# Gated delta rule: the inverse of the chunk triangle from 16x16 blocks instead of 8x8, and the side work of a head in another order

## What is computed

```python
def _gated_delta(q, k, v, beta, g):            # per head, in chunks of 64 tokens
    gc = jnp.cumsum(chunks(g), axis=-1)
    decay = jnp.where(incl, jnp.exp(jnp.where(incl, diff, 0.0)), 0.0)
    kb = k * beta[..., None]
    lower = jnp.where(strict, jnp.einsum('bhncd,bhned->bhnce', kb, k) * decay, 0.0)
    tri = lower + jnp.eye(GDN_CHUNK)
    rhs = jnp.concatenate([v * beta[..., None], kb * jnp.exp(gc)[..., None]], axis=-1)
    sol = lax.linalg.triangular_solve(tri, rhs, left_side=True, lower=True, unit_diagonal=True)
    u, w = sol[..., :d], sol[..., d:]
    intra = jnp.einsum('bhncd,bhned->bhnce', q, k) * decay
    def step(state, xs):
        v_new = u_i - w_i @ state
        o = qh_i @ state + intra_i @ v_new
        state = state * exp(gl_i) + kt_i.T @ v_new
```

## Time and profile before

| | |
|---|---|
| median of three runs | 2551.5 us (2549.22 to 2552.22) |
| the profiled execution: its own time | 2552.11 us |
| its span, first to last instruction | 2550.3 us |
| mean granted PE clock | 0.979 of full |
| busy: PE, POOL, DVE, ACT | 2360.8, 1320.1, 1397.3, 591.1 us |
| gated-delta stages | about 577 to 995 us and 1783 to 2197 us of the span |
| moved from and to HBM | 316 MB, 124 GB/s on average |

### The profile page before, as it was taken

One profiled execution on the slowest core, in us unless ns is written; L12 is line 12 of the kernel. 1 busy time (PEld: TensorE's weight loads), 2 busy tenths in 40 slices (PEclk: granted clock), 3 DMA queues, 4 the chain that ended last, 5 costly groups with the idle time before them and its releaser, 6 DMA issues.

```text
span 2550.3 us, 36954 instructions
## 1 busy us (share of the span) xinstructions
PE 2360.8 (93%) x13312; PEld 1891.9 (74%) x13312; DVE 1397.3 (55%) x2112; ACT 591.1 (23%) x1150; POOL 1320.1 (52%) x1018
## 2 busy tenths in 40 slices
PE   0898999998999999999998999999899999999996
PEld 0666777786777777777876788788677777887885
DVE  8964654656666664665126255155666665234536
ACT  0211210222223332222023122022222222224001
POOL 6673357434444444656655644644444444554763
PEclk9998999998999999999999999999999999999998
DMA  9864346321122213454325532532122222222542
GB/s 360 303 218 168 117 157 249 127 93 58 60 67 67 67 61 120 150 190 162 98 68 200 179 116 94 198 110 78 57 67 67 67 67 67 67 83 67 182 141 91
DMA packets 94595, 316.01 MB, mean 124 GB/s; under 512 B 10918, under 2 KB 11174, under 8 KB 93382
## 3 DMA queue, kind: packets, MB, share of 16 engines
q1 hardware_dynamic: 86768, 295.48, 33.7%
q10 hardware_dynamic: 7644, 18.16, 2.1%
HBM read 303.89 MB, written 8.39 MB: 122 GB/s over the span
## 4 chain that ended last, share of the span: by engine, by line
PE 71%; DVE 16%; POOLq 3%; ACT 3%; issue 3%; DMA 2%; POOL 1%; DVEq 1%; ACTq 1%; SPq 0%
PE bank L651 14%; PE bank L653 14%; PE bank L652 14%; DVE arena L1709 12%; PE bank L1172 4%; PE bank L1174 4%; PE bank L1173 4%; DVE acc L1709 3%; PE bank L961 2%; PE bank L932 2%; ACT arena L1202 1%; POOLq L1651 1%; POOL w_lo L1649 1%; PE bank L953 1%; DVEq L1710 1%
## 5 line engine op out<-in xcount | busy, mean ns | idle before, releaser
L1645 POOL CAST w_hi<-ring 128x1024 fp32r<-128x1024 f32 (+1 forms) x320 | 353.8, 1106 | 1098.5 <-PE bank L653 916.0
L1649 POOL TENSOR_TENSOR w_lo<-ring,w_hi 128x512 fp32r<-128x512 f32 (+1 forms) x632 | 885.1, 1421 | 48.5 <-issue 1.3
L651 PE MATMUL bank<-h_hi,w_hi 128*128 128x512 f32 x1952 | 826.5, 423 | 10.3 <-POOLq L1651 8.4
L653 PE MATMUL bank<-h_hi,w_lo 128*128 128x512 f32 x1952 | 773.1, 396 | 0.0
L652 PE MATMUL bank<-h_lo,w_hi 128*128 128x512 f32 x1952 | 769.5, 394 | 0.0
L651 PEld LDWEIGHTS bank<-h_hi,w_hi 128*128 128x128 f32 x1952 | 372.7, 191 | 95.4 <-issue 15.6
L653 PEld LDWEIGHTS bank<-h_hi,w_lo 128*128 128x128 f32 x1952 | 371.2, 190 | 84.6
L652 PEld LDWEIGHTS bank<-h_lo,w_hi 128*128 128x128 f32 x1952 | 373.0, 191 | 72.5 <-issue 7.2
L1202 ACT ACTIVATE arena<-bank 128x512 f32<-128x512 f32 (+5 forms) x360 | 169.3, 470 | 668.9 <-PE bank L653 216.6
L1709 DVE SCALAR_TENSOR_TENSOR acc<-yT,cact,acc 128x1024 f32<-128x1024 f32 (+1 forms) x144 | 209.6, 1455 | 37.3 <-DMA acc<-in_b_mod 14.2
L1172 PE MATMUL bank<-w_hi,h_hi 128*128 128x512 f32 x448 | 175.6, 392 | 0.5 <-issue 0.5
(11 more groups left out here) (230 smaller groups left out, 2828.4 us busy)
## 6 DMA issues: line engine op xcount, KB each, us to landing
ring<-in_stream SPq DMA_DIRECT2D x352, 512.0 KB, 3.5
yT<-in_stream SPq DMA_DIRECT2D x128, 512.0 KB, 4.6
yT<-in_mod SPq DMA_DIRECT2D x32, 1024.0 KB, 7.9
arena<-in_x ACTq DMA_DIRECT2D x4, 1024.0 KB, 9.7
x_norm<-arena ACTq DMA_DIRECT2D x4, 1024.0 KB, 8.1
arena<-x_norm ACTq DMA_DIRECT2D x4, 1024.0 KB, 10.0
out<-arena SPq DMA_DIRECT2D x3, 1024.0 KB, 3.9
arena<-in_x SPq DMA_DIRECT2D x1, 2048.0 KB, 13.9
```

What stands on the lines that cost most here:

```text
L651: mm(PJ[b][:, :], hi, h_hi[:, k, :], start=(k == 0), stop=False)
L653: last = mm(PJ[b][:, :], lo, h_hi[:, k, :], start=False, stop=(k == KT - 1))
L1645: pool.tensor_copy(w_hi[:, par, 0:w], ring[:, slot, 0:w])
L1649: pool.tensor_tensor(w_lo[:, par, at], ring[:, slot, at], w_hi[:, par, at].bitcast(F32), ALU.subtract)
```

## The change

It makes the substitution over 16x16 blocks: 14 steps instead of 6, on tiles of 16 columns for each chunk. The level of 8 is dropped, so PE, ACT and DVE merge twice, and then once more for the whole chunk. The running inverse and the broadcast row lie in a PSUM bank, TB[1], which has held the key product until then; the reduced triangle and the products lie in the second half of `A(14)`. The copies `lT_swapped`, which nobody reads, are gone.

The order of the side work is another. On DVE, the substitution stands directly behind the triangle; `intra`, `mask(1)` and `both_squares` stand behind the assembly; the tail of the head before stands behind the first update; v and `conv_k0` behind the second; `conv_k1` behind the `own` copies; the scaling of v behind the `cross` block; the coefficients of the next head are copied by a part of their own (`coef`) behind that; `key` and `weigh` stand at the end of the recurrence. On PE, the turning of `intra` (`gdn_iT`) and the tail of the head before are moved behind the first update and the second product, the turning of v to `REC - 2`; the fill is another, 25 k-steps between the key product and the first merge, 2 in the recurrence where there were 3. On ACT, the tail stands behind the copy of the first product, with the tanh of v behind it; the copy of `intra`, the tanh of z and the square of q stand behind the second product; ACT's copy of w waits for DVE's product with z; `tanh_q` and `norm_k` come one chunk later.

```diff
-BASE = 8
-LEVELS = (8, 16, 32)
+BASE = 16
+LEVELS = (16, 32)
...
         base_l, base_x, base_row, base_part = (
-            A(11)[:, NW + i * NB:NW + (i + 1) * NB].rearrange("p (t n) -> p t n", t=TT) for i in range(4))
-        lT_n, lT_swapped = narrow(A(12)), narrow(A(12)[:, NW:])
+            ap[:, i * NB:(i + 1) * NB].rearrange("p (t n) -> p t n", t=TT)
+            for ap, i in ((A(14)[:, NW:], 0), (TB[1], 0), (TB[1], 1), (A(14)[:, NW:], 1)))
+        lT_n, lv_n = narrow(A(12)), narrow(A(12)[:, NW:])
...
-        gdn_fill = [5, 6, 5] + [3, 3, 2, 3, 2, 3, 2, 3, 2] + [2, 3, 2, 3, 3, 3, 3, 3, 3]
+        gdn_fill = [5, 9, 9] + [7, 3, 2, 3, 2, 3, 2] + [2, 2, 2, 2, 3, 2, 2, 2, 2]
...
                         if s == 1:
-                            ready("gdn_egb")
                             ready("gdn_lower")
                             transposes(MB, A(3)).then_inc(S("gdn_lT"), 1)
-                            if not first:
-                                tail(h - 1)
-                        if s == 2:
-                            ready("gdn_lT_copied")
-                            ready("gdn_intra")
-                            transposes(MB, A(17)).then_inc(S("gdn_iT"), 1)
...
+                                if v == len(LEVELS) - 1:
+
+                                    pe.wait_ge(S("gdn_T"), D * 2 * len(LEVELS) + 2 * v + 1)
+                                    transposes(MB, A(17)).then_inc(S("gdn_iT"), 1)
...
-                                if v == 1:
-
-                                    pe.wait_ge(S("y_ready"), after("y_ready", l * 16 + NSA_H + h))
-                                    ready("gdn_v")
-                                    transposes(OB, A(10)).then_inc(S("gdn_vT"), 1)
+                                if v == 0 and not first:
+                                    ready("gdn_egb")
+                                    tail(h - 1)
...
                                 if v == 0:
+                                    if not first:
+                                        tail(h - 1)
+                                    act.wait_ge(S("gdn_conv"), D * 3 + 3)
+                                    fn(A(5), A(10), ACT.Tanh, scale=0.5).then_inc(S("gdn_vtanh"), 1)
+                                if v == len(LEVELS) - 1:
+                                    ready("gdn_iT")
+                                    fn(A(16), MB[:, :], ACT.Copy).then_inc(S("gdn_i_copied"), 1)
+                                    fn(A(18), raw[:, 3, TAPS - 1:], ACT.Tanh, scale=0.5).then_inc(S("gdn_ztanh"), 1)
                                     front(h, "square_q")
-                                if v == 2 and not last:
+                                if v == N_LEVELS - 1 and not last:
                                     front(h + 1, "tanh_k")
                         if s == REC - 1:
                             ready("gdn_w")
+                            act.wait_ge(S("raw_used3"), after("raw_used3", l * N_LOTS + h + 1))
                             fn(A(18), TB[0][:, :], ACT.Copy, scale=-1.0).then_inc(S("gdn_w_copied"), 1)
...
                     tt(A(3), TB[1][:, :], A(2), M).then_inc(S("gdn_lower"), 1)
-                    if not first:
-                        both_squares(h - 1)
-                    ready("gdn_qk")
-                    tt(A(17), SB_[0][:, :], A(17), M).then_inc(S("gdn_intra"), 1)
-
-
-                    tt(tiles(A(14)), tiles(A(3)), over(C("base_lower").unsqueeze(1), BIG), M)
-                    reduce(base_l, A(14).rearrange("p (t b n) -> p t n b", t=TT, n=BASE), AX, Ad)
+
+                    tt(tiles(A(11)), tiles(A(3)), over(C("base_lower").unsqueeze(1), BIG), M)
+                    reduce(base_l, A(11).rearrange("p (t b n) -> p t n b", t=TT, n=BASE), AX, Ad)
...
-                        if j == BASE - 2:
+                        if j == BASE // 2:
                             ready("gdn_lT_copied")
                             mask(0)
...
                     sync().then_inc(S("gdn_T"), 1)
 
+                    ready("gdn_qk")
+                    tt(A(17), SB_[0][:, :], A(17), M).then_inc(S("gdn_intra"), 1)
                     mask(1)
-                    ready("gdn_vtanh")
-                    stt(A(10), A(5), 1.0, A(10), Ad, M).then_inc(S("gdn_v"), 1)
+                    if not first:
+                        both_squares(h - 1)
+                    dve.wait_ge(S("gdn_TCT"), D * (len(LEVELS) + 2) + 1)
+                    tt(inv_n, inv_n, narrow(SB_[0]), Su).then_inc(S("gdn_T"), 1)
+                    tt(invT_n, invT_n, narrow(MB), Su).then_inc(S("gdn_T"), 1)
...
+                    ready("gdn_vtanh")
+                    stt(A(10), A(5), 1.0, A(10), Ad, M).then_inc(S("gdn_v"), 1)
                     if not last:
                         front(h + 1, "conv_k0")
...
                     sync().then_inc(S("gdn_Tt"), 1)
+                    if not last:
+                        front(h + 1, "conv_k1")
+                    dve.wait_ge(S("gdn_TCT"), D * (len(LEVELS) + 2) + 4)
+                    ts(cross(inv_T), narrow(SB_[0])[TOP], -1.0, None, M).then_inc(S("gdn_Tt"), 1)
+                    ready("gdn_vT")
+                    tt(tiles(A(8)), tiles(OB[:, :]), per_token(2), M).then_inc(S("gdn_Tt"), 1)
+                    if not last:
+                        front(h + 1, "coef")
                     ready("gdn_ztanh")
                     stt(A(19), A(18), 1.0, raw[:, 3, TAPS - 1:], Ad, M).then_inc(S("raw_used3"), 1)
...
                         if not last:
-                            front(h + 1, ("silu_q", "conv_v", "decay", "weigh")[i])
-                            if i == 1:
-                                front(h + 1, "key")
+                            front(h + 1, ("silu_q", "conv_v", "decay", "key")[i])
+                            if i == TT - 1:
+                                front(h + 1, "weigh")
```

More of the change, by code:

```diff
@@ L1071, in delta @@
                                 if not last:
-                                    front(h + 1, ("norm_k", "decay", None, None)[i])
+                                    front(h + 1, (None, "norm_k", "decay", None)[i])
                             else:
@@ L1473, in delta @@
                                 fn(lT_n[(TOP, LOW)[half]], own(MB, half), ACT.Copy)
-                                fn(lT_swapped[(LOW, TOP)[half]], own(MB, half), ACT.Copy)
                             fn(lastT, cross(MB), ACT.Copy).then_inc(S("gdn_lT_copied"), 1)
-                            if not first:
-                                tail(h - 1)
-                        if s == 2:
-                            ready("gdn_iT")
-                            fn(A(16), MB[:, :], ACT.Copy).then_inc(S("gdn_i_copied"), 1)
-                            act.wait_ge(S("gdn_conv"), D * 3 + 3)
-                            fn(A(5), A(10), ACT.Tanh, scale=0.5).then_inc(S("gdn_vtanh"), 1)
-                            fn(A(18), raw[:, 3, TAPS - 1:], ACT.Tanh, scale=0.5).then_inc(S("gdn_ztanh"), 1)
                         for v in range(N_LEVELS):
@@ L1499, in delta @@
                                 front(h + 1, "square_k")
-                                front(h + 1, "tanh_q")
                         if REC <= s < GDN_STEPS - 1 and (s - REC) % 2 == 0:
@@ L1971, in front @@
                         conv(h, 0, 0, 1, 0, 2)
+                    if part == "coef":
+                        one_head = slice(h, h + 1)
+                        cp(coef_h[:, :, :], coef[:, :, :, one_head].rearrange("p a t h -> p (a t) h").rearrange(
+                            "p (a t) h -> p a (t h)", t=TT)).then_inc(S("gdn_coef"), 1)
                     if part == "conv_k1":
@@ L2099, in delta @@
                         tail(h)
-                for part in ("conv_k0", "conv_k1", "conv_q0", "silu_k", "conv_q1", "silu_q", "key", "conv_v", "decay", "weigh"):
+                for part in ("coef", "conv_k0", "conv_k1", "conv_q0", "silu_k", "conv_q1", "silu_q", "key", "conv_v", "decay", "weigh"):
                     front(0, part)
```

46 lines of the change are left out of this document (17 added, 29 removed).

## The result

The changed kernel takes 2520.1 us, the median of four runs (2514.6 to 2522.7), against 2551.3 us (2549.2 to 2552.2, four runs) for the kernel before on the same chip. The ratio is 0.987, 95% interval 0.9857 to 0.9884. That is 31.2 us less; the forecast was 30.3 less, at 2521.

A forecast was written before the change was run, and what follows sets the result against it. PE's own stream was taken to bound the kernel, with 2.07 us of stall in a steady head. The terms, 22.3 + 19.7 + 3.0 - 13.5 - 1.2 = 30.3 us less, gave 2521 us, range 2507 to 2538.

The forecast's parts named there:

- the new waits: Behind the first merge and up to the first state, moved side work makes PE wait 1.35 us in ten heads, 13.5 us.
- the level: Dropping the 8-level's product and update takes 1.64 us a head off PE, 19.7 us in 12 heads.
- the first heads: First head of each layer: inverse 4.3 us later against 4.2 us of extra k-steps, net zero.
- the half clock: Behind the stall in the second and fifth of ten heads, PE's half clock goes: some 1.5 us each, 3 us.
- The stall: PE's wait at the first merge for the block inverse goes in ten heads, 22.3 us; inverse 2.3 us ahead of PE.
- The step of the substitution: DVE's block inverse: 14 steps of a shuffle and two small products, 0.87 us each and even, 12.2 us in all.
- rivals B and C: B: operations with a bank input 0.25 us, 2533, chance 0.12. C: DVE's bank writes, 0.35 us an operation, 2598, chance 0.04.
- POOL and two SBUF inputs: In the substitution, small DVE operations with two SBUF inputs stall beside POOL's subtractions; with one in a bank, 0.18 us.
- rival A: Waits moved, not removed: DVE's stretch from last update to first state limits, 3 us in ten heads, 2538, chance 0.18.
- Heads 62 to 62.5 us apart: Sign that the forecast is right: successive heads are 62 to 62.5 us apart.
- Rival D: The new waits don't come, DVE and POOL falling out of step: 13.5 us back, 2508, chance 0.12.
- The stall that stays: At the first merge the longer substitution eats the longer cover; the stall stays at 2 us: 2547, chance 0.04.

The follow-up runs named there:

- Experiment 3: Changed kernel with conv_k0 moved ahead of DVE's wait for the first update (2512.0 us), then conv_k1 also moved, behind v (2497.0 us).
- e3: Changed kernel with 14 k-steps ahead of the first merge instead of 25, the other 11 in the recurrence: 2586.7 us.
- e1: Changed kernel with the running inverse and the broadcast row in SBUF instead of the PSUM bank: 2602.9 us.
- e8: Changed kernel with the running inverse in SBUF and only the broadcast row in the bank: 2557.2 us.
- e4: Changed kernel with 8x8 blocks and three levels again, 20 k-steps ahead of the first merge: 2531.8 us.
- e9: Changed kernel with conv_k0 and conv_k1 moved early, 8x8 blocks, three levels and 20 k-steps ahead of the first merge: 2510.7 us.
- e5: Changed kernel with conv_k0 moved ahead of DVE's wait for the first update and conv_k1 from behind the own copies to behind v: 2497.0 us.
- e7: Changed kernel with two k-steps moved from ahead of the first merge (25 to 23) to behind the last update: 2502.1 us.

## Why the prediction was right, and where not

The forecast of 2521 met 2520.1. The mechanism was right, but that the number came within 1 us is luck: the new waits took more than forecast (18.4 us by the list, against 13.5), the level gave 1.3 less, and the first heads and the half clock, 5.6 and 2.6 us more than forecast, and 2.5 us at L1051 and 1.2 us in the last heads, which it had not counted on, made up for it.

- **The stall, 22.3 us in ten heads: right.** No steady head waits at the merge. The inverse came at 18.2 us instead of 17.6: an "issue" gap of 0.4 us and the mask between two steps (0.69 at 671.74, taken as 0.5). The reserve was 1.6 us, not 2.3. Experiment 3's e3 shows what hides the longer substitution: without the eleven k-steps the kernel is slower than before.
- **The step of the substitution, 0.87 us and even: right**, 0.83 to 0.93, but for the two steps around the mask. The value taken for an operation on a bank, 0.18 us, is 0.168 to 0.229 as measured, from 128x8 to 128x60; at 128x16 the product that writes a bank takes 183 ns, the one that writes SBUF 175, and one with everything in SBUF 176 (e1). With this rivals B and C fall. The page "VectorE: DVE Perf Modes" of the Trainium skill, section "The TRN2 errata", has 120 cycles of fixed cost from PSUM against 58 from SBUF. The rows here show no such difference: 175 ns for 128x16 with a bank input, 176 ns with two SBUF inputs. The same section has the formula (N+151)/0.96 for a fp32 `tensor_tensor`, checked there at 512 and 2048 elements; it gives 174 ns at 16 and 220 at 60, and the trace agrees with it at either place.
- **POOL and two SBUF inputs: right as a cause, too small as a size.** The page "SBUF — State Buffer" of the Trainium skill, section "Who interferes with whom", says that a DVE instruction with two SBUF inputs contends with a GpSimd instruction that reads SBUF, and one with a single such input, outside the two-port modes, doesn't. By e1 and e8 the trace agrees: the small operation lasts as long as the subtraction (1.27 us) or the cast (1.04 us) beside it.
- **The level, 1.64 us a head: 1.5** by the distance of the heads of e4 and of e9. I read it off as the whole distance less the column products; why that is 0.1 too much wasn't followed.
- **The new waits, 1.35 us a head: 1.75, and elsewhere.** This is the term that was mis-sized. Three guesses made it. The cross block and ACT's copy of w were given 0.6 and 0.3; the cross block cost 0.42 and the copy nothing. The copy on ACT behind the tail was given 0.4 and cost nothing: PE doesn't wait for it in any head. The first state was called "nearly level" and cost 1.33. The failed step is the balance of that stretch: the prediction set DVE 1.4 us behind against a PE reserve of 1.04 (1.39 less the state's 0.35) and then looked for waits in between. Its own terms give 1.1 for it (2.8 less 3.9), and measured it is 2.7: the first state is updated 3.14 us after kv starts (703.23 to 706.37), where before it was 0.42 (710.15 to 710.57). DVE's stretch from the last update to the state was 13.3 us, 2.8 of them its wait for kv, and is 15.3 now: 4.8 us more of its own, and not 3.9. And PE reaches kv 12.2 us after that update started where it took 12.9, not "about the same distance". Of DVE's 4.8 us, 1.17 is one change that wasn't foreseen: the three conv products of q just before the state took 2.94 us in the second head before (0.75 and 2.19), and take 4.11 now, since POOL's subtractions (704.02 to 707.24) have moved onto them. So rival A's mechanism is real and decides the limit of this kernel, at 18.4 us instead of its 30. The 1.2 us given to the tails of the two last heads never came: PE doesn't wait at L986, the product behind the squares. The sign of "a single wait over 1 us at the first state" was the right one to name.
- **The first heads, "net zero": a gain of 5.6 us.** The prediction set six more k-steps (4.2 us) against an inverse 4.3 us later. By the fill there are eleven more: three ahead of the triangle's wait and eight behind it, 7.6 us. It had read the 2.66 us wait at the triangle and given it no term, and the three k-steps cover it: L637 fell from 5.3 to 0.6. At the merge itself the two heads wait 1.86 and 5.05 where they waited 3.44 and 4.3, so "near 4 us or above" held in one of the two.
- **Half clock, 3 us: 5.6.** I had counted the second and the fifth head, 1.5 us each, and there the size was right; the two heads behind the first merges of a layer, 67.66 and 66.42 us long before, had it too.
- **Heads 62 to 62.5 us apart: 63.1.** This is the cleanest miss. With the waits away heads are 60.9 (e5) and 60.8 (e7) apart, so the new waits cost 2.2 to 2.3 us a head and not 1.35. That is more than the 1.75 in the list, because a wait is counted from the modelled end of the product before it: at the state two starts are 1.72 us apart (705.06, 706.78) that were 0.22 apart before, 1.50 for a wait of 1.33. PE's own stream was forecast at 61.2 and is 0.3 shorter; 0.25 of that is the waits at L1051, which it had counted as stream.
- **Rival D**, no new waits at all, gave 2508; e7 and e5 are 6 and 11 us below it; the first heads (5.6) and the half clock (2.6 more than forecast), which the sum left out or put too low, are of that size.
- **The stall that stays (2547)** would have needed a longer chain; e8, whose inverse comes 4.0 us later in a steady head (1.6 of reserve and 2.42 of wait), is at 2557.

## What to carry to other kernels

Before a chain of small VectorE operations is made longer, look where its operands lie and what GpSimd does at the time: here a chain of 42 operations of 0.2 us hides behind PE with its running tile and its row in PSUM, and costs 83 us with both in SBUF. A cover bought with filler is taken from somewhere: look for the engine's next stretch without reserve, begin it at the last point at which that engine still has to wait, and move work out from behind that point alone. When one stall is cured, write down the reserve that is left there: here the kernel was faster when both ends had just enough (2 k-steps moved were worth 18 us).

## What the runs showed of the hardware

- A DVE operation of 48 bytes a partition with both inputs in SBUF took 1.06 us on average beside POOL's 1.27 us subtractions, and 0.17 us with one input in a bank. It lasts until POOL's operation beside it ends, whatever its own size, and a cast of POOL holds it as well (a pair of 128x24 took 1.15 us beside a cast of 1.04, 0.44 free).
- Reads and writes of a bank by DVE cost within 8 ns what those of SBUF cost, for these sizes: 168 to 229 ns; a shuffle of 128x64 within a bank took 233 ns, 228 within SBUF.
- Behind every one of the 24 waits at the merge in e1 and e3 (5.1 us and more) PE's clock was at the half level for some of the next column products (0.43 us apart, 0.23 at full). Behind the waits of 2.06 to 2.61 us before, it was so in two of ten heads, and cost some 1.5 us each time.
- The stalls repeat to 0.01 us from head to head (2.42 in nine of ten heads in e8, 2.43 in the tenth), so one head's timeline is enough, except for the first of a layer.
